# A two-branch encoder step on one core: x laid out by token thirds, the first heads' operands built under the value product, and new places for cache tiles and normalisation

## The reference, cut to what matters

```python
proj = x @ w_in                       # q, k, v, forget logits | GLA parts | branch gates
logf = log_sigmoid(fa + b_fgate)
# branch A, 8 heads x 64: softmax(q k / 8 + C[t] - C[s]) v, C = cumsum(logf), causal
#   sample sequences attend to 256 cached keys and values of their own and to their 16 tokens
# branch B: gated linear attention, 4 heads
merged = sigmoid(ga) * (oa @ w_a_out) + sigmoid(gb) * (ob @ w_b_out)
x1 = LN(ALPHA * x + merged @ w_o)
# then a convolutional feed-forward, LN, a gated embedding, LN
```

## Time and profile before

| what | value |
| --- | --- |
| median of 3 runs | 2519.25 us (2517.82 to 2524.0) |
| the profiled execution, its own time | 2524.86 us |
| its span | 2523.2 us |
| PE busy | 2350.7 us, 93% |
| share of PE in the chain that ended last | 85% |
| DVE busy | 1280.0 us, 51% |
| ACT busy | 672.4 us, 27% |
| POOL busy | 225.2 us, 9% |

### The profile page before, as it was taken

The page is one execution under the profiler, slowest core; times in us unless marked ns, Lnnn a source line. Parts: engine busy times, 40 slices in busy tenths (PEclk is TensorE's granted clock), DMA queues, the critical chain, the costliest instruction groups (busy, mean ns, idle before and its releaser), DMA issues.

```text
span 2523.2 us, 31967 instructions
## 1 busy us (share of the span) xinstructions
PE 2350.7 (93%) x13127; PEld 2155.7 (85%) x13127; DVE 1280.0 (51%) x1696; ACT 672.4 (27%) x1077; POOL 225.2 (9%) x412
## 2 busy tenths in 40 slices
PE   7996998789999999999999989999999999999697
PEld 6995776588888888899999879999999999998585
DVE  3113663236363636200243285767767767666685
ACT  3111664133333333211122122221221221221311
POOL 0001000000101010100013020000000000000431
PEclk8997999899999999999999999999999999999798
DMA  4114543411212121211211400111111111110210
GB/s 135 42 42 121 157 107 104 150 48 34 72 34 72 34 71 34 100 43 38 101 55 51 159 17 26 51 42 34 50 46 35 46 50 36 40 42 27 110 51 34
DMA packets 154432, 160.29 MB, mean 64 GB/s; under 512 B 14058, under 2 KB 127014, under 8 KB 153158
## 3 DMA queue, kind: packets, MB, share of 16 engines
q1 hardware_dynamic: 147958, 132.94, 18.0%
q0 software_dynamic: 6368, 25.84, 2.8%
HBM read 122.26 MB, written 23.84 MB: 58 GB/s over the span
## 4 chain that ended last, share of the span: by engine, by line
PE 85%; DVE 5%; DMA 2%; ACT 2%; issue 2%; POOL 2%; SPq 1%; DVEq 0%; ACTq 0%; POOLq 0%
PE ps L565 73%; PE ps L820 2%; PE ps L900 2%; PE ps L708 2%; PE ps L668 1%; DMA sb<-in_cache_fox_k 1%; PE ps L690 1%; DVE sb L1362 1%; PE ps L691 1%; DMA ring_raw<-in_w_in 1%; DVE sb L1449 1%; POOL sb L1933 1%; DVE sb L1704 1%; PE ps L669 1%; POOL sb L1905 0%
## 5 line engine op out<-in xcount | busy, mean ns | idle before, releaser
L1011 ACT ACTIVATE sb<-ps 128x384 f32<-128x384 f32 (+6 forms) x312 | 128.8, 435 | 868.6 <-PE ps L565 783.4
L565 PE MATMUL ps<-x_hi,up_hi 128*128 128x384 f32 x1056 | 354.3, 336 | 0.3 <-DVE x_lo L1721 0.3
L565 PE MATMUL ps<-x_hi,up_lo 128*128 128x384 f32 x1056 | 354.2, 335 | 0.0
L565 PE MATMUL ps<-x_lo,up_hi 128*128 128x384 f32 x1056 | 353.8, 335 | 0.0
L1776 DVE TENSOR_TENSOR sb<-sb,ps 128x512 f32<-128x512 f32 x396 | 270.9, 688 | 117.7 <-PE ps L565 117.3
L565 PE MATMUL ps<-x_hi,ring_hi 128*128 128x384 f32 x960 | 322.8, 336 | 3.4 <-DVE x_lo L1380 3.4
L565 PE MATMUL ps<-x_lo,ring_hi 128*128 128x384 f32 x960 | 321.4, 335 | 0.0
L565 PE MATMUL ps<-x_hi,ring_lo 128*128 128x384 f32 x960 | 321.3, 335 | 0.0
L1372 DVE TENSOR_TENSOR ring_lo<-ring_raw,ring_hi 128x1024 fp32r<-128x1024 f32 (+1 forms) x68 | 78.3, 1160 | 334.4 <-ACT ring_hi L1011 333.9
L565 PEld LDWEIGHTS ps<-x_hi,up_hi 128*128 128x128 f32 x1056 | 198.8, 188 | 3.2 <-DVE x_lo L1721 0.7
L565 PEld LDWEIGHTS ps<-x_lo,up_hi 128*128 128x128 f32 x1056 | 198.8, 188 | 2.5
(11 more groups left out here) (263 smaller groups left out, 4235.6 us busy)
## 6 DMA issues: line engine op xcount, KB each, us to landing
ring_raw<-in_w_in SPq DMA_DIRECT2D x52, 512.0 KB, 3.9
up_raw<-in_w_up SPq DMA_DIRECT2D x44, 512.0 KB, 3.9
sb<-in_x_prompt SPq DMA_DIRECT2D x24, 512.0 KB, 6.9
down_raw<-in_w_down SPq DMA_DIRECT2D x22, 512.0 KB, 4.6
branch_b<-sb POOLq DMA_DIRECT2D x4, 1152.0 KB, 8.2
ob_raw<-branch_b POOLq DMA_DIRECT2D x4, 1152.0 KB, 9.7
out<-sb POOLq DMA_DIRECT2D x9, 512.0 KB, 3.0
kk<-k_hi SPq DMA_DIRECT2D x16, 256.0 KB, 4.3
```

The source lines that it names most:

```text
L565: m = mm(out, l, r, start=(n == 0), stop=(n == len(pairs) - 1))
L1011: return act.activation(out, in_, ACT.Copy, scale=scale)
```

## The change

x is kept as [third][k tile][384 tokens], so that a third of it takes the first, second or third 3072 floats of R1 and of R2. The operand sets and the attention's buffers are placed so that set 0 lies in the first third (with `kc0`, `qhi`, `khi` in the first third of the low part), set 1 in the second, and the rest of set 2 and the exponentials in the last. The turns of the log-forgets and of k stand between the tiles of the first half of the value product. POOL clears set i after tile 3i+2 of the second half, ACT splits q and k of heads 0 and 1 after tile 2, and SP issues the operands of heads 0 and 1 at once, before it waits for the value product; the stores of v and of the log-forgets and head 2 come after. The second pair is split at step 1 of head 0.

The cache tiles 0 to 7 each have a buffer of their own: keys 4 to 7 go into set 2 while head 6 runs, values 0 to 3 into ring slots 2 and 3, values 4 to 7 into set 0 while head 7 runs. With the latter, x tiles 0 to 3 are loaded into the memory of v, before SP's store of the chunk (6, 1); the other x tiles follow after the last step. Weight chunks 12 and 13 are loaded after the stores of k, 14 and 15 after `sample_v(3)`. The normalisation moves to POOL: it issues its transfers on its own queue and multiplies, for pairs 0 to 2 within the attention and before it clears `qbd`, for pair 3 between the `qbd` copies; DVE inverts the row sums of a pair after step 0 of heads 3, 5 and 7 and in the sample stage. The diff, cut to its core:

```diff
-        place(off["early"], ("kp", 4096), ("ost", 512))
+        place(off["early"], ("kp0", 1024), ("kp1", 1024), ("kp2", 1024), ("kp3", 1024), ("ost", 512))
...
-        place(off["R1"], ("set0", 4096), ("set1", 4096), ("set2", 4096), ("e0", 1024), ("e1", 1024), ("ph0", 1024),
-              ("ph1", 1024), ("qhi", SEQ), ("khi", SEQ))
+        place(off["R1"], ("qq0", SEQ), ("kk0", SEQ), ("qc0", SEQ), ("qq1", SEQ), ("kk1", SEQ), ("qc1", SEQ),
+              ("qc2", SEQ), ("kc2", SEQ), ("e0", 1024))
+        place(off["R2"], ("kc0", SEQ), ("qhi", SEQ), ("khi", SEQ), ("kc1", SEQ), ("qq2", SEQ), ("kk2", SEQ),
+              ("e1", 1024), ("ph0", 1024), ("ph1", 1024))
         off["e2"], off["ph2"] = off["kT"], off["qT"]
-        place(off["set0"], ("qbd", 1312), ("kpT", 2048), ("sN", 256))
-        place(off["set1"], ("sP", 768), ("sPT", 768), ("om", 1024), ("oas", 512))
-        place(off["set2"], ("vp", 4096))
+        place(off["qq1"], ("sP", 768), ("sPT", 768), ("om", 1024), ("oas", 512))
+        off["kpT"] = off["qhi"]
+        for i, name in enumerate(("qq2", "kk2", "qc2", "kc2")):
+            off[f"kp{i + 4}"] = off[name]
+        for i, name in enumerate(("qq0", "kk0", "qc0", "kc0")):
+            off[f"vp{i + 4}"] = off[name]
+        place(off["ring"] + 2048, ("vp0", 1024), ("vp1", 1024))
+        place(off["ringh"] + 2048, ("vp2", 1024), ("vp3", 1024))
+        for i in range(2):
+            place(off["qT"] + (2 + i) * T, (f"qbd{i}", 656), (f"sN{i}", P))
...
-        xh, xl = rounded("x_hi", off["xh"], KT, T), rounded("x_lo", off["xl"], KT, T)
+        xh, xl = rounded("x_hi", off["xh"], 3, KT, THIRD), rounded("x_lo", off["xl"], 3, KT, THIRD)
+        def x_tile(x, n):
+            return x[:, n // 3, :, n % 3 * P:(n % 3 + 1) * P]
...
-        oab, rbb = ([at(off[n], 1024) for n in names] for names in (("e0", "ph0", "qhi"), ("e1", "ph1", "khi")))
+        oab = at(off["qT"] + T, 1024)
+        rbb = [at(off["kT"] + T, 1024)] * 3 + [at(off["e0"], 1024)]
...
+            def turn_logf():
+                pe.wait_ge(s_lf8, 1)
+                o = take(pe, "lfT")
+                for n in range(NT):
+                    m = tr(o[:, n * H_A:(n + 1) * H_A], fz[:, n * P:(n + 1) * P], ident[0:H_A, 0:H_A])
+                m.then_inc(filled("lfT"), 1)
+            def turn_k(n):
+                if n == 0:
+                    copied(pe, *[("ka", j, g) for j in range(4) for g in range(3)])
+                o = take(pe, ("kt", n))
+                for j in range(4):
+                    m = tr(o[:, j * P:(j + 1) * P], kT[:, j, n * P:(n + 1) * P], ident)
+                m.then_inc(filled(("kt", n)), 1)
             for q in range(2):
                 weights(pe, ("va", 2 * q + 1))
                 for n in range(NT):
                     o = take(pe, ("va", q, n))
                     pair_tile(o, ("va", 2 * q), n).then_inc(filled(("va", q, n)), 1)
+                    if q == 0:
+                        if n == 0:
+                            turn_logf()
+                        turn_k(n)
...
-            for q in range(2):
-                for n in range(NT):
-                    o = product(act, ("va", q, n))
-                    copy(va[:, n, q * 256:(q + 1) * 256], o[:, 0:256]).then_inc(drained(("va", q, n)), 1)
-                if q == 0:
-                    split_hi(11, 12)
...
-            past_pe(act, ("va", 1, NT - 1))
-            copied(act, *[("qa", 0, g) for g in range(3)])
-            act.wait_ge(s_const, 16)
             copy(idr, ident)
             copy(causr, causal).then_inc(s_hi, 1)
-            qk_hi(0)
-            act.wait_ge(s_lo, 2)
-            qk_hi(1)
-            act.wait_ge(s_pz, 10)
+            for q in range(2):
+                for n in range(NT):
+                    o = product(act, ("va", q, n))
+                    copy(va[:, n, q * 256:(q + 1) * 256], o[:, 0:256]).then_inc(drained(("va", q, n)), 1)
+                    if (q, n) == (0, 2):
+                        split_hi(11)
+                    if (q, n) == (1, 2):
+                        copied(act, *[("qa", 0, g) for g in range(3)])
+                        qk_hi(0)
+                if q == 0:
+                    split_hi(12)
+            copied(act, *[("va", 1, n) for n in range(NT)])
+            act.wait_ge(s_pz, 4)
...
+                    if t == 1:
+                        qk_hi(1)
...
-            split_hi(13, 14)
+            split_hi(13)
...
+            split_hi(14)
...
-            split_lo(11, 12)
...
+                if n == 3:
+                    split_lo(11)
+            split_lo(12)
...
+            def row_scale(j):
+                dve.wait_ge(s_rsi, 80 * j + 16)
+                dve.reciprocal(rinv[:, 16 * j:16 * (j + 1)], rsum[:, 16 * j:16 * (j + 1)]).then_inc(s_oan, 1)
...
-            qk_lo(1)
...
+                if t == 1:
+                    qk_lo(1)
...
+                if s == 0 and h in (3, 5, 7):
+                    row_scale((h - 3) // 2)
+            split_lo(13)
             for b in range(DEC_B + 3):
-                if b == 1:
-                    dve.wait_ge(s_rsi, 16)
-                    dve.reciprocal(rinv, rsum).then_inc(s_oan, 1)
-                if b in (3, 4, 5):
-                    norm_pair(b - 3)
-                if b == 7:
-                    norm_pair(3)
+                if b == 2:
...
+                    row_scale(3)
...
+            split_lo(14)
...
-            past_pe(pool, ("va", 1, NT - 1))
-            for i in range(3):
-                pool.memset(sets[i][2][64:P, :].bitcast(F32), 0.0).then_inc(s_pz, 1)
-                pool.memset(sets[i][3][64:P, :].bitcast(F32), 0.0).then_inc(s_pz, 1)
-            pool.wait_ge(s_pz, 6)
             for i in range(2):
                 pool.memset(VH[i][:, :, DH:DH + 1].bitcast(F32), 1.0).then_inc(s_pz, 1)
                 pool.memset(VL[i][:, :, DH:DH + 1].bitcast(F32), 0.0).then_inc(s_pz, 1)
-            pool.wait_ge(s_pz, 10)
             for i in range(3):
+                pool.wait_ge(s_pz, 4 * i + 4)
+                past_pe(pool, ("va", 1, 3 * i + 2))
+                pool.memset(sets[i][2][64:P, :].bitcast(F32), 0.0).then_inc(s_pz, 1)
+                pool.memset(sets[i][3][64:P, :].bitcast(F32), 0.0).then_inc(s_pz, 1)
+                pool.wait_ge(s_pz, 4 * i + 6)
                 pool.memset(sets[i][2][64:66, :].bitcast(F32), 1.0).then_inc(s_pz, 1)
                 pool.memset(sets[i][3][96:98, :].bitcast(F32), 1.0).then_inc(s_pz, 1)
             pool.wait_ge(s_pz, 16)
+            def row_sums(j):
+                pool.wait_ge(s_oas2, 128 * (j + 1))
+                pool.dma_start(rsum[:, 16 * j:16 * (j + 1)], rs_out[2 * j:2 * j + 2].rearrange("h (a n) -> (h a) n", n=16))\
+                    .then_inc(s_rsi, 16)
+            def row_scales(j):
+                pool.wait_ge(s_oan, j + 1)
+                pool.dma_start(ri_out[2 * j:2 * j + 2].rearrange("h (a n) -> (h a) n", n=16), rinv[:, 16 * j:16 * (j + 1)])\
+                    .then_inc(s_rsi, 16)
+            def load_pair(j):
+                pool.wait_ge(s_rsi, 80 * j + 32)
+                if j:
+                    pool.wait_ge(s_oao, 16 * j)
+                pool.dma_start(oab, oa_out[:, j, 0:SEQ]).then_inc(s_rsi, 16)
+                for e in range(2):
+                    pool.dma_start(rbb[j][e * DH:(e + 1) * DH, :], ri_out[2 * j + e].partition_broadcast(DH))\
+                        .then_inc(s_rsi, 16)
+            def store_pair(j):
+                pool.wait_ge(s_rsi, 80 * (j + 1))
+                pool.tensor_tensor(oab, oab, rbb[j], ALU.mult).then_inc(s_oam, 1)
+                pool.wait_ge(s_oam, j + 1)
+                pool.dma_start(oa_out[:, j, 0:SEQ], oab).then_inc(s_oao, 16)
+            for j in range(3):
+                row_sums(j)
+                row_scales(j)
+                if j == 0:
+                    set_in(pool, 2)
+                    set_in(pool, 3)
+                load_pair(j)
+                store_pair(j)
             pool.wait_ge(s_s2, NS * (H_A - 1))
-            pool.memset(at(off["qbd"], 1312), 0.0).then_inc(s_pool, 1)
-            pool.wait_ge(s_pool, 1)
+            for i in range(2):
+                pool.memset(qbd[i], 0.0).then_inc(s_pool, 1)
...
+                if b == 1:
+                    row_sums(3)
+                if b == 2:
+                    row_scales(3)
+                if b == 3:
+                    load_pair(3)
+                if b == 4:
+                    pool.wait_ge(s_qbd, b + 1)
+                    store_pair(3)
...
-            for n in range(4, 16):
+            for n in range(4, 12):
                 load(n)
-            copied(sp, *[("va", q, n) for q in range(2) for n in range(NT)])
...
+            load(12)
+            load(13)
...
+                if h < 3:
+                    sp.wait_ge(s_pz, 4 * h + 8)
...
-            sp.wait_ge(s_pz, 16)
-            for h in range(3):
-                head_operands(h)
+            head_operands(0)
+            head_operands(1)
```

(53 more changed lines are left out.)

68 lines of the change are left out of this document (27 added, 41 removed).

## The result

The changed kernel takes 2480.45 us in the median (2478.44 to 2482.13, 4 runs) where the kernel before takes 2521.25 (2517.82 to 2524.0, 4 runs): a ratio of 0.9839, 95% interval 0.9821 to 0.9856, 40.8 us faster. The forecast was 2462.0 with a range of 2455 to 2477; the sign was right, the size was not. The profiled execution took 2480.09 us, its span is 2478.4, so the two spans differ by 44.8 us where 57.0 were forecast.

The account below looks back on a forecast made before the run. PE was taken as the bound, busy 93% of the span, so only its idle or low-clock time could be won. First part 31.6 plus second part 25.4 gave 57.0 us off 2519.25: 2462, range 2455 to 2477.

Parts of the forecast that it names:

- Row scores start early: Into the attention: row scores start near 208.5 instead of 231.17, head 0's operands being ready under the value product; 22.7 us.
- The 1.6 us charged to a stall's half clock: Value product's second half: 1.6 us lost to half speed behind the 2.7 us weight-chunk stall, expected to go with it.
- Row scores at full clock: Row scores and turn of the maxima: 15.7 us at clock 0.50 become 10 at full clock; 5.7 us.
- The rival that puts the clock down to new holes: End of head 7 and sample-stage start: clock falls in holes of some 4 us; 5.5 once or twice, chance 0.14.
- the rival on the slower side: From the row scores on: half clock stays, heads and sample sequences run cold; 28 slower, 2547, chance 0.02.
- Heads 0 to 2: Head 0 at full clock takes 19.7 instead of 24.1, 4.4 won; second pair's split and head 2's operands cost 1.2.
- Store (0, 1): Early heads: the store stands behind a burst of v but is due some 4 us after landing; cost nothing.
- Lock of VectorE and GpSimd: Attention: POOL late, or locked with DVE's p_lo subtractions, its loads slowed by the burst; 5 to 10 us, chance 0.09.
- The sample stage: PE's 17.7 us of waits for cached tiles and 11.1 of half clock go with all tiles loaded before; 28.8.
- The last head: End of head 7: the new order makes the first sample scores begin near 411, 3.4 late (bounds 0 and 10).
- Term (a): Last head: store (6, 1) lies behind eight 512 KB transfers, so ACT's next chunk copy comes 4.0 late (bounds 0, 4.9).
- the first rival: Clock falls in the new holes at head 7's end and the sample stage's start; 2468 to 2473, chance 0.14.

Follow-up runs that it names:

- e14: Kernel before, with only the nine transfers of x moved behind cached keys 6 on SyncE; 2522.16 us, ratio 1.0000 to the kernel before.
- e16: Kernel before, SyncE reordered: all four late cached keys ahead of its waits for the normalisation and of x, no new homes; 2491.77 us, ratio 0.9883.
- e13: Kernel before, with x moved behind keys 6 and keys 4 ahead of the loads of pairs 0 to 2; 2526.08 us, ratio 1.0013.
- e8: Changed kernel, with SyncE waiting for the whole value product to be copied out before it issues head 0's operands; 2494.32 us.
- e1: Changed kernel plus 18 unread TensorE matmuls: among head 0's row scores and around the turn of the maxima; 2478.70 us.
- e2: Changed kernel plus only the nine unread matmuls between head 0's row scores; 2479.38 us.
- e7: Changed kernel, with loads of cached values and x behind the last stores, and qbd built for sequences 0 and 1 before pair 2; 2476.74 us.
- e3: Changed kernel, with the four loads of cached values issued behind store (0, 1) instead of ahead of it; 2474.49 us.
- e4: Changed kernel, with pairs 0 and 1 multiplied by their row scales on VectorE at step 4 of heads 4 and 6, not on GpSimd; 2487.66 us.
- e10: Changed kernel, with pairs 0 and 1 multiplied by their row scales on VectorE at step 0 of heads 4 and 6, not on GpSimd; 2478.40 us.
- e11: Changed kernel, with cached keys and values of sequences 4 to 7 loaded in the sample stage instead of early, homes kept; 2475.82 us.
- e5: Changed kernel, last head: four loads of cached values moved behind store (7, 0), first four of x behind store (7, 1); 2477.47 us.
- e6: Changed kernel, with GpSimd clearing qbd and building it for sequences 0 and 1 before it handles pair 2; 2479.46 us.

## Why the forecast was right and wrong

The spans differ by 44.8 us. By the forecast's own steps, measured minus forecast:

- **Row scores start early** (22.7): 23.4, +0.7. That it came so close is in part luck: the profiled execution of before starts them late, and against e14 and e16, where the code up to there is the same, it would be 20.5 and 19.8. The 1.6 us charged to a stall's half clock in the value product belonged to the execution and not to the kernel (PEclk 0.94 in 180 to 207.3 us, as in e13, but 1.00 in e14 and e16, which have the same stall of 2.68). The value product's second half ran without the stall of the earlier trace rows, and SP issued head 0's operands while it ran. Undoing this part costs 13.9 us of the whole (e8).
- **Row scores at full clock** (5.7): 2.4, -3.3. This step failed: "PE enters it from a full value product, so I take 10". It entered at full clock and lost it some 7 us later. No run shows the 9.3 us of the sum: e1, at 1.00 throughout, takes 11.85 with its added matmuls. The sum leaves PE idle a third of the time, and e1 and e2 show that with this idle time filled the clock does not fall there. The rival that puts the clock down to new holes had 0.14, and only for the end of the attention; the rival on the slower side named this place, with 0.02, and took the clock never to rise again.
- **Heads 0 to 2** (4.4 for head 0, less 1.2): 62.8 us before, 66.5 after, so -3.7 instead of +3.2, -6.9 in all. Of these, 5.2 lie in head 0, which still ran at half clock (23.86; e1 at 1.00 takes 18.61, which is the 4.4 of the forecast), and 1.7 in heads 1 and 2. But full clock alone would not have brought them: the other step that failed is "Store (0, 1) is issued behind a burst of v as well, but is due only some 4 us after it would land: nothing". It landed 1.4 us too late in the changed kernel, and 4.2 too late once head 0 was fast (e1). I priced the operands of head 2, keys, operands of head 3, values and the store singly; in the traces of e1 and e7 they are one chain of SP's issues and landings, started by the split of the second pair (in e7 it runs from 227.76 to 265.82, 38 us), and in the changed kernel that chain holds from 244.92 on. Half a clock above it cost almost nothing by itself (e1: 1.3 us), and removing the burst alone gave 2.9 (e3).
- **Lock of VectorE and GpSimd** (a rival, 0.09): it happened, though to `v_lo` and not to the `p_lo` that was priced, and for 1.2 us, not 5 to 10. `v_lo` took 2.90 instead of 0.69 at 304.99 and at 345.91, and the first cost head 4 1.2 us (e4, e10). The rule of the Trainium skill (SBUF — State Buffer, "SBUF: two separate sides"), that of such a pair of operations the one that starts first has the shared ports for its whole instruction, agrees with these rows, starts and lengths added up: both `v_lo` end 0.56 and 0.55 us behind POOL's multiplication, and both multiplications end 2.26 us behind the `p_lo` that had begun before them (POOL alone takes 2.35).
- **The sample stage** (28.8): 103.2 to 73.6, 29.6, +0.8. The size was right and its reason was not. "With all tiles loaded before the stage both go" names the early loads; e11 shows that they aren't needed, e16 that another order on one queue is enough. I read a wait for a load as a load triggered late, and did not ask what SP itself was waiting for ahead of it. The 28.3 us of e16 and the 13.9 of e8 add up to 42.2, beside the 40.8 of the whole change.
- **The last head** (-3.4): -5.1, -1.7. Term (a), the store behind the burst, was right: ACT's copy 4.0 late by the forecast, 3.34 in the trace, and PE behind it waits 3.97. Two followers were left out of the sum and stand only among the rivals: half clock from about 385 to 392 (the first rival, 0.14), and POOL's pair, held up by the same burst (e5). POOL's stored scales took 4.58 us to land by its wait, where the sum had 1.5.
- **The rest of the kernel** (0): -0.6.

0.7 - 3.3 - 6.9 - 1.2 + 0.8 - 1.7 - 0.6 is -12.2, which is 44.8 against 57.0. The other 6.2 us of the miss in the time (18.45) come from the reference: the profiled execution of before was 5.6 us above the median I started from, the one of after was 0.4 below its own, 0.2 is rounding, and I took a sum made on that one execution off the median.

Of the kernel before's 5.6 us the record shows a part: up to the first sample scores its profiled execution is 2.1 us behind e14's and 5.4 behind e16's, which run the same code there, 1.6 of it from the lower clock in the value product. Open is why the clock falls at 208.8 us in e7, between 212.9 and 214.6 in the changed kernel, e3, e4, e5, e6 and e11, and at 215.9 in e10, although their code is the same there; head 0 takes 21.5 in the earliest and the latest, 23.8 to 24.1 in the others.
